# Routing the next group of a PEER mixer during the score stage: piece borders shifted by 14 slots

## What is computed

```python
def trunk_layer(x, ...):
    proj = rmsnorm(x, norm_mix) @ w_in      # split: rg_x, rg_gate, ssd_z, ssd_xbc, ssd_dt, merge
    rg_y = rg_lru(causal_conv(rg_x), ...)   # linear recurrence over tokens
    y_a = (rg_y * gelu(rg_gate)) @ w_rg_out
    y = ssd_chunked(silu(causal_conv(ssd_xbc)), dt, ...)      # chunks of 128 tokens, state carried
    y_b = rmsnorm((y + D*xs) * silu(ssd_z)) @ w_ssd_out
    x = x + (sigmoid(g_a) * y_a + sigmoid(g_b) * y_b) @ w_out
    x = x + peer(rmsnorm(x, norm_ffn))

def peer(t):                                # 8 heads, 2 x 128 keys, top 16, 16384 experts
    s = keys . (t @ w_q)                    # scores, 2 sets of 128 for each head
    sv, si = top_k(s, 16)                   # for each set
    fv, fi = top_k(sv[0][:, None] + sv[1][None, :], 16)
    idx = si[0][a] * 128 + si[1][b]         # 16 experts for each token and head
    act = gelu(u_emb[idx] . t)
    return sum(softmax(fv) * act * v_emb[idx])
```

## Time and profile before

| | us |
|---|---|
| median of 3 runs | 2421.6 |
| lowest, highest | 2417.84, 2428.31 |
| the profiled execution | 2434.43 |
| its span, first to last instruction | 2432.6 |

### The profile page before, as it was taken

The page is one execution under the profiler, slowest core; times in us unless marked ns, Lnnn a source line. Parts: engine busy times, 40 slices in busy tenths (PEclk is TensorE's granted clock), DMA queues, the critical chain, the costliest instruction groups (busy, mean ns, idle before and its releaser), DMA issues.

```text
span 2432.6 us, 30812 instructions
## 1 busy us (share of the span) xinstructions
PE 1724.4 (71%) x10511; PEld 1181.5 (49%) x10511; DVE 1596.3 (66%) x4212; ACT 496.4 (20%) x1460; POOL 926.5 (38%) x840
## 2 busy tenths in 40 slices
PE   7899966677798989877899899995534434434343
PEld 7799966422686866655678666672100000000000
DVE  5634178777458533988666775635187888778864
ACT  3345233100134122222222340110011000010000
POOL 0000001144334442543444555556644544444442
PEclk9999988656899989998899999997666555666666
DMA  7387756279999997885799999998999999999995
GB/s 247 127 273 251 240 165 207 87 267 349 352 376 352 387 380 268 320 310 178 284 388 355 366 357 384 388 394 294 360 421 422 422 421 421 421 418 413 406 422 239
DMA packets 179629, 798.80 MB, mean 328 GB/s; under 512 B 20721, under 2 KB 20977, under 8 KB 143505
## 3 DMA queue, kind: packets, MB, share of 16 engines
q0 software_dynamic: 119808, 570.48, 60.2%
q1 hardware_dynamic: 57312, 219.39, 24.9%
q10 hardware_dynamic: 2352, 6.95, 1.0%
HBM read 779.88 MB, written 12.14 MB: 326 GB/s over the span
## 4 chain that ended last, share of the span: by engine, by line
PE 19%; DMA 13%; DVE 11%; issue 5%; POOL 3%; ACT 1%; POOLq 0%; DVEq 0%; SPq 0%
PE ps L471 10%; DMA s_exr<-in_uv,s_gidx 7%; PE ps L776 3%; DVE s_exr L1650 3%; DMA s_wr<-in_uv,s_gidx 2%; PE ps L759 2%; PE ps L454 2%; DMA s_hnr<-in_uv,s_gidx 1%; POOL s_exr L1307 1%; DMA s_scr<-in_uv,s_gidx 1%; POOL s_exr L1262 1%; DVE s_wr L1650 1%; POOL s_exr L1274 1%; DMA s_exr<-in_v,s_gidxT 1%; PE ps L796 1%
## 5 line engine op out<-in xcount | busy, mean ns | idle before, releaser
L471 PE MATMUL ps<-s_hnr,s_wr 128*128 128x128 f32 (+2 forms) x4224 | 719.5, 329 | 68.4 <-ACT s_hist_p L935 38.8
L471 PEld LDWEIGHTS ps<-s_hnr,s_wr 128*128 128x128 f32 x4224 | 648.4, 199 | 150.1 <-issue 98.3
L1262 POOL DMA_INDIRECT s_exr<-in_u,s_gidx x288 | 316.0, 1097 | 894.1 <-DVE s_act_z L1650 454.8
L1650 DVE CUSTOM_DVE_ANT_0 s_exr<-s_exr,s_tbg 128x1024 f32<-128x1024 f32 x407 | 491.9, 1221 | 175.4 <-DMA s_exr<-in_u,s_gidx 101.9
L1274 POOL DMA_INDIRECT s_exr<-in_v,s_gidxT x256 | 281.6, 1100 | 214.8 <-PE ps L759 105.4
L776 PE MATMUL ps<-s_exr,s_sw 128*32 128x512 f32 x476 | 153.7, 1022 | 167.6 <-DVE s_sw L1679 162.7
L1307 POOL DMA_INDIRECT s_exr<-in_uv,s_gidx x119 | 137.3, 1154 | 147.8 <-PE ps L776 117.5
L759 PE MATMUL ps<-s_exr,s_zb 128*32 128x512 f32 x1072 | 152.2, 676 | 47.5 <-DMA s_exr<-in_v,s_gidxT 44.4
L776 PEld LDWEIGHTS ps<-s_exr,s_sw 128*32 128x32 f32 x476 | 24.9, 156 | 246.2 <-DVE s_sw L1679 187.9
L776 PE MATMUL ps<-s_scr,s_sw 128*32 128x512 f32 x160 | 89.0, 1042 | 61.9 <-DVE s_sw L1679 61.9
L776 PE MATMUL ps<-s_wr,s_sw 128*32 128x512 f32 x152 | 84.2, 1033 | 66.1 <-DVE s_sw L1679 66.1
(11 more groups left out here) (310 smaller groups left out, 2627.5 us busy)
## 6 DMA issues: line engine op xcount, KB each, us to landing
s_wr<-in_wstream SPq DMA_DIRECT2D x360, 512.0 KB
s_tbg<-s_h2e ACTq DMA_DIRECT2D x36, 128.0 KB
s_exr<-in_u,s_gidx POOLq DMA_INDIRECT x288
s_exr<-in_v,s_gidxT POOLq DMA_INDIRECT x268
s_xr<-in_sample_h_in SPq DMA_DIRECT2D x4, 1024.0 KB
s_scr<-in_sample_h_in SPq DMA_DIRECT2D x4, 1024.0 KB
out_sample_h_out<-s_xr SPq DMA_DIRECT2D x4, 1024.0 KB
out_sample_h_out<-s_scr SPq DMA_DIRECT2D x4, 1024.0 KB
```

The lines of the kernel that those rows point to most:

```text
L471: last = pe.matmul(ps[:, o % 2, 0:n], wring[:, slot, k, :], rhs[:, k, :], start=k == 0, stop=k == KT - 1)
L1262: pool.indirect_dma_start(uring[n % URING], None, a["u"], bass.IndirectOffsetOnAxis(ap=gidx[:, i % 2, s:s + 1], axis=0)).then_inc(u_in[n % ...
L1650: dve.tensor_tensor_reduce(out=u, in0=u, in1=tbg[:, i % 2, :], scale=1.0, scalar=0.0, op0=ALU.mult, op1=ALU.add, accum_out=act_z[:, i % 2, ...
```

## The change

The route of the first group of a piece moves to slots 21, 22, 23, 24 (first half) and 27, 28, 29, 30 (second half) of groups 3 and 8, and the dense steps of a piece now end at slot 26 of that group, not at 12. The first half therefore needs only two of the four quarters of the scores, and its wait is written so. The exponentials follow at slots 23 and 29. ScalarE's exponential for the dt row of pieces 1 and 2 stands one unit earlier: else it would stand behind the exponential of slot 29, whose input VectorE gives only after the dt row is through, and the two engines would wait for each other.

```diff
-EDGE_SLOT = 15
+EDGE_SLOT, EDGE_END = 21, 26
@@ due_slots
-        end = SLOTS * EDGE[pc.p - 1] + EDGE_SLOT - 3 if pc.p else 0
+        end = SLOTS * EDGE[pc.p - 1] + EDGE_END if pc.p else 0
@@ scalar, slot
-                        if s == (EDGE_SLOT + 4 + 8 * j if i in EDGE else 6 + 11 * j):
+                        if s == (EDGE_SLOT + 2 + 6 * j if i in EDGE else 6 + 11 * j):
                             softmax_exp(2 * (i + 1) + j)
@@ scalar, xbc
-                    if n == 2:
+                    if n == (1 if p else 2):
                         act.wait_ge(sp_in, p + 1)
                         act.activation(pc.sp[1], pc.sp[2], ACT.Exp).then_inc(sp_exp, 1)
@@ vector, route_keys
-                if j == 0 and s == 0:
+                if i in FIRST and s == 0:
+                    dve.wait_ge(sc_ready, 4 * GROUPS[i][0] + 2 * (j + 1))
+                elif j == 0 and s == 0:
                     dve.wait_ge(sc_ready, 4 * (GROUPS[i][0] + 1))
@@ vector, slot
-                    first, step, gap = (EDGE_SLOT, 8, 2) if i in EDGE else (2, 11, 2)
+                    first, step, gap = (EDGE_SLOT, 6, 1) if i in EDGE else (2, 11, 2)
```

More of the change, by code:

```diff
@@ L134 @@
 DUE = due_slots()
+assert all(DUE[(p, "wq", 9)] <= SLOTS * EDGE[p - 1] + EDGE_SLOT for p in (1, 2))
 class Pace:
```

## The result

The kernel after takes 2397.6 us in the median of 7 runs (2392.43 to 2405.48), the kernel before 2421.6 beside it (7 runs, 2413.39 to 2428.31): a ratio of 0.9895 with an interval of 0.9872 to 0.9918, 24 us faster. The forecast was 2415, 7 us faster; its range held the result, its likeliest case ("no change that can be told") and its own range of 2403 to 2428 did not.

The account below looks back on a forecast made before the run. Memory was taken to bound the stream from group 9 on; before it, dense stages bound by VectorE or TensorE and a tail of GpSimd gathers. Dense part +32 and tail -39 gave -7 from 2421.6, say 2415 us; range 2395 to 2435.

Parts of the forecast that it names:

- Tail, -39: Last scores to first dot of group 9: 8 gathers left instead of 32, first dot 39 us earlier, bounds 34 and 43.
- part 2: The route's price: 10.9 us of VectorE a half, covered at border 1 (end of piece 1); border 2's wait costs nothing.
- part 1: The tail before group 9's first dot becomes shorter: 39 us earlier.
- The old rows: The 32 old v rows gathered in the tail, 1711.3 to 1757.4, stay; dots beside them might give back up to 4 us.
- Border 1 covered with 10 us to spare: End of piece 1, group 3: first half and four dots, 16 us, fit under VectorE's 26.0 us wait for the root.
- Piece 1, +25.5: Dense stages and score stage of piece 1 with 14 more slots: 25.5 us longer.
- the check from the other side: Piece 1 from piece 0's scaled time, eight sequences at 9 us each: slots cost 1.8 us each, 14 of them 25.
- Piece 2, +7: Dense stages of piece 2 slide by 14 slots against the groups: 4 - 2 + 5 = 7 us, bounds 0 and 12.
- The score stage, 0.5: Score stage of piece 1: two more slots beside an idle VectorE cost 0.5 us, bounds 0 and 5.
- the covered slots: Rival: gathers and dots mostly covered in piece 1, which costs 12, piece 2 nothing: -27 us, about 2395; chance 0.30.
- The memory-bound rival: Memory stream bounds piece 1, each moved slot costs 2.7 us: +15 us, about 2437; chance 0.18.
- The late half: Rival: first half not done under the score stage, old rows wait for VectorE: some 10 us lost, about 2425; chance 0.06.

Follow-up runs that it names:

- e2: Kernel after, but only piece 2 ends at slot 26 (of group 8); piece 1 ends at slot 12 of group 3: ratio 0.9954 to the kernel before.
- e4: Kernel after, unchanged, run and profiled again in set 1: ratio 0.9926 to the kernel before.
- e1: Kernel after with the route at its new slots, but pieces ending at slot 12 as before: 2391.7 us against 2397.7 for the kernel before, ratio 0.9979.
- the first pair: The first profiled executions of the kernels before and after, unchanged: 2434.43 and 2392.43 us.
- e5: Kernel before, unchanged, run and profiled a second time in set 2: ratio 0.9983.
- e11: Kernel after plus 25 repeats of a MAX8 on VectorE at slot 21 of group 3: 2385.5 us against 2380.0 for the kernel after.
- e7: Kernel after with group 2's route, in group 1, at slots 20 to 27 instead of 2 to 19, behind seq: ratio 0.9876 to the kernel before.
- e8: Kernel after with group 8's route, in group 7, at slots 10 to 16 and 18 to 24, first half out of sr: ratio 0.9866 to the kernel before.
- e9: Kernel after with three routes (in groups 1, 5 and 7) moved to later slots: 2361.1 us against 2380.0 for the kernel after.
- sets 1 and 3: Two of three sets of follow-up runs beside the kernel before, on different chips; the kernel before took 2397.7 and 2397.0 us in them.
- e10: Kernel after, but 34 gathers beside samp and seq of piece 1 fetch 64 of 128 partitions: ratio 0.9940 to the kernel before.

## Why the prediction was right or wrong

- **Tail, -39.** Measured -42 (108.9 to 67.1), and the mechanism as written: 8 gathers, 13.5 us for 12 by the price, the release 6.1 us earlier where I took 3. e2 shows it as border 2's, and e4 against e1, without the route's move, has -38.6. Up to 3 of the 42 come with the route's new slots (the wait for a dot in before): part 2 left the gain of that move to part 1, which held 3 for it, since I asked who waits behind the new wait and hardly who was held by the old one.
- **The old rows.** They "stay", as I had it, where nothing else disturbs them: 41.2 us in e1 and in e4. In the first pair they took 4 us less, since before has a wait of 5.8 us in them that is not the kernel's (`remote`, see e5). By the rule of the Trainium skill (GPSIMD Engine Reference, Key points) dots should have lengthened them. The first pair's trace agrees in part: the 32 issues take 32.4 us for 30.8, with 1.17 us in the mean for the 8 into s_wr (1.04 before) against 0.94 for the 12 into s_exr; e4 against e1 shows 31.5 for 31.4. My price was read one-sidedly: beside the same dots the u gathers of the earlier trace rows have 937 ns in the median, like the old rows, and only the means of both kinds (1.19 and 1.18 us) lie above.
- **Border 1 covered with 10 us to spare.** Covered for the most part, and nothing to spare: the wait of 26.0 was the longest of five executions (5.9 to 26.0), with 19.0 us of ScalarE's `remote` waits in its stage; after has none left, and e11's 9.8 us cost 5.5. From the end of the last query copy to the first copy of xbc it is 13.0 to 16.8 us in the three executions of after, 13.3 and 14.8 in those of before: some 1 us came through in the mean. The cover was read from one profile, 13 us above its median.
- **Piece 1, +25.5.** Measured +25 (means of four and four), 1.8 us for a slot. Right as a sum and as a price. Its parts were less so (after against e5): xbc, ssd and seq together grew by 13 us (310.1 against 296.9), not 17, since seq covers four fifths or so of the route (e7); sr by 6 for 5; gb, z, ga and wo by 5 for 3. That these errors cancel is luck, and the check from the other side rests on 9 us for a sequence that no row gives.
- **Piece 2, +7.** Measured -1.5 (means of three executions of after, 629.9, and two of before, 631.4), and -2 for e4 against e1; nothing that can be told from 0. After against e5, sr grew by 8 and the start with xbc by 3, and ssd, gb with z, and all from ga on gave back 2, 2 and 5. I had put what gb, z and wo give back at nothing, since VectorE is no limit there, without a row for it. By e8 and e9, sr's growth is not the route's, so counting route halves by stage gave 5 of the 8 there for a wrong reason; it does hold in ssd (e9).
- **The score stage, 0.5.** Right between kernels of one set (e1 120.9, e4 119.6 for both). In the first two profiles 19 us lie here (144.6 and 125.3), and no term of the sum stands for them; they are waits that come and go with the execution.
- **The signs.** In the first pair piece 1 up to its last query copy did not grow (636.1 to 634.7 us), which I had named as a sign of being wrong, and the last scores came at 1656.6 and not 25 to 40 us later than 1660.8. Both are those same 19 us, 18 of them in piece 1: e4 against e1 has 638.8 for 607.3, and its last query copy 24 us later. The other signs came: 8 gathers, 67 us, 668 us; the wait for the root was 0 and not near 10.
- **The sum.** With the measured terms, +25 and -1.5 against 42 give -18.5; sets 1 and 3 show -18 and -17 (2397.7 to 2380.0, 2397.0 to 2380.0). The forecast of -7 misses that by piece 2's 8.5 us and the tail's 3. Another 6 of the 24 in the first comparison fit the score stages, without proof. So the step that failed is the size of piece 2's term, and its bound: 0 was the lower end, without a reason against a gain.
- **The rivals.** The time came near that of the covered slots (2395), but not by its mechanism: slots in piece 1 paid their 1.8 us. That the range, whose lower end was this rival's time, held 2397.6 is luck as well. The memory-bound rival fell: seq does not feel a fifth of its bytes (e10), gb and z took 388 GB/s and ga and wo 409 in piece 1. The figure of about 358 GB/s in the Trainium skill (DMA: Bandwidth & Descriptors, Where 436 GB/s comes from) is passed by each of these rows. The late half did not come about; it costs 3.9 us of one gather.

## What to carry to other kernels

Take the price of a moved step from the stage where it lands, and try it by moving that one step out: half a route was worth 14 us in ssd, a fifth of its own time in seq, and nothing in gb and z. When a wait moves, ask who was held by it where it stood, as well as who it will hold. And when a median and a profile disagree by as much as the expected effect, read the cover from a second profile before it is spent, and look in both for waits that no instruction released: they are not the kernel's to spend.

## What was not expected of the hardware

- The mean busy share of the DMA engines did not fall with the bytes: 0.94 at 351 GB/s and 0.93 at 277 (e10). A share near 1 is no sign that bytes are the limit.
- Removing VectorE work from a chain shortened it by more than the work: 9.3 us less of VectorE, 14.3 us less of stage, with TensorE's granted clock at 0.92 for 0.85 and 5.7 us less of its busy time (e9). TensorE's waits for VectorE in it fell from 28.5 to 17.9 us; no run here varied the clock alone, so how much of the 14.3 is the clock's stays open.
- The same program took 2397 us in two sets and 2429 in a third, and the profiles put most of it into the two score stages (119 to 126 us against 125 to 145), at 309 to 347 GB/s in piece 2's against 396. With it come waits of up to 14.6 us that end at no instruction of the core: 26 to 60 us in each of six executions, none in the eight others. Their cause stays open.
